# A DeltaNet / RWKV-7 / PEER decoder step: RWKV matrices directly behind the z tiles, gate tiles redistributed, inversion units by chunk

## Time and profile before

| | |
|---|---|
| runs shown | 1148.66 (median), 1147.56, 1153.62 us |
| the profiled execution's own time | 1150.32 us |
| its span | 1148.6 us |
| PE busy | 982.6 us (86%) |
| DVE busy | 706.5 us (62%) |
| POOL busy | 521.4 us (45%) |
| ACT busy | 264.1 us (23%) |
| mean granted TensorE clock | 0.978 of full |

### The profile page before, as it was taken

How to read it: one execution, slowest core, us unless ns; L and a number is a source line. 1 busy time by engine, 2 the same in 40 slices (tenths; PEclk the granted TensorE clock), 3 DMA queues, 4 the chain that set the end, 5 groups by cost and what they waited for, 6 DMA issues and landing times.

```text
span 1148.6 us, 11115 instructions
## 1 busy us (share of the span) xinstructions
PE 982.6 (86%) x3667; PEld 549.7 (48%) x3667; DVE 706.5 (62%) x1870; ACT 264.1 (23%) x635; POOL 521.4 (45%) x583
## 2 busy tenths in 40 slices
PE   6999998999999998988987777777777777777787
PEld 5886676889987447654442222222222222222221
DVE  2025862983466338883775775776686676677543
ACT  2147544023251012220131111111122111111111
POOL 2000100000000016577577677777767777777763
PEclk9998989998999998998999999999999999999999
DMA  9342022463165319999999999999999999999996
GB/s 288 110 153 74 1 76 50 135 171 82 40 208 208 110 46 405 407 371 353 409 406 403 409 409 409 406 408 408 408 388 410 409 409 410 405 409 404 395 371 263
DMA packets 121862, 334.24 MB, mean 291 GB/s; under 512 B 19119, under 2 KB 36370, under 8 KB 121542
## 3 DMA queue, kind: packets, MB, share of 16 engines
q0 software_dynamic: 76032, 276.86, 61.2%
q1 hardware_dynamic: 45642, 56.64, 15.2%
q10 hardware_dynamic: 132, 0.04, 0.0%
HBM read 326.99 MB, written 5.74 MB: 290 GB/s over the span
## 4 chain that ended last, share of the span: by engine, by line
PE 31%; DMA 28%; DVE 23%; POOL 9%; issue 5%; ACT 3%; ACTq 0%; DVEq 0%; POOLq 0%
PE bank L1428 29%; DMA sb_all<-in_peer_u,idx 22%; POOL sb_all L591 9%; DMA sb_all<-in_peer_v,idx 6%; DVE sb_all L1148 6%; ACT sb_all L1846 2%; DVE sb_all L1126 1%; DVE sb_all L1124 1%; DVE sb_all L1128 1%; DVE sb_all L2337 1%; DVE sb_all L2334 1%; DVE key_i L1096 1%; DVE sb_all L1089 1%; ACT L1846 1%; DVE key_i L1090 1%
## 5 line engine op out<-in xcount | busy, mean ns | idle before, releaser
L1428 PE MATMUL bank<-sb_all 128*128 128x512 f32 (+19 forms) x3390 | 952.3, 433 | 145.8 <-DMA sb_all<-in_peer_v,idx 135.6
L1428 PEld LDWEIGHTS bank<-sb_all 128*128 128x128 f32 (+8 forms) x3390 | 522.9, 182 | 569.7 <-DMA sb_all<-in_peer_v,idx 320.4
L1148 DVE CUSTOM_DVE_ANT_0 sb_all<-sb_all,bank 128x1024 f32<-128x1024 f32 x264 | 314.8, 1220 | 186.5 <-DMA sb_all<-in_peer_u,idx 186.0
L591 POOL DMA_INDIRECT sb_all<-in_peer_u,idx x264 | 252.6, 957 | 212.4 <-issue 161.1
L591 POOL DMA_INDIRECT sb_all<-in_peer_v,idx x264 | 254.6, 965 | 88.8 <-issue 63.8
L1846 ACT ACTIVATE sb_all<-sb_all 128x128 f32<-128x128 f32 (+9 forms) x367 | 145.1, 421 | 561.7 <-PE bank L1428 368.6
L1846 ACT ACTIVATE sb_all<-bank 128x264 f32<-128x264 f32 (+18 forms) x175 | 76.7, 455 | 305.2 <-PE bank L1428 272.0
L627 POOL MEMSET sb_all<- 128x512 f32 x1 | 0.5, 524 | 140.9 <-PE bank L1428 140.9
L1418 POOL MEMSET sb_all<- 128x3456 f32 x1 | 3.0, 2984 | 129.1 <-DVE sb_all L2248 129.1
L2129 DVE SCALAR_TENSOR_TENSOR sb_all<-sb_all 128x288 f32<-128x288 f32 x14 | 6.1, 514 | 61.2 <-ACT sb_all L1846 61.2
L1846 ACT ACT_TABLE_LOAD x22 | 28.2, 1283 | 7.5 <-DVE sb_all L2269 3.9
(11 more groups left out here) (237 smaller groups left out, 403.5 us busy)
## 6 DMA issues: line engine op xcount, KB each, us to landing
sb_all<-in_w_in SPq DMA_DIRECT2D x8, 2048.0 KB, 8.1
sb_all<-in_peer_wq SPq DMA_DIRECT2D x4, 2048.0 KB, 17.3
sb_all<-in_w_in SPq DMA_DIRECT2D x6, 1024.0 KB, 4.9
sb_all<-in_peer_u,idx POOLq DMA_INDIRECT x264, 10.8
sb_all<-in_peer_v,idx POOLq DMA_INDIRECT x264, 11.0
out<-sb_all SPq DMA_DIRECT2D x8, 512.0 KB, 3.9
sb_all<-in_w_out SPq DMA_DIRECT2D x2, 2048.0 KB, 8.6
sb_all<-in_x_prompt SPq DMA_DIRECT2D x4, 512.0 KB, 4.4
```

The lines of the kernel that those rows point to most:

```text
L591: pool.indirect_dma_start(ring[at % 8], None, table[0], bass.IndirectOffsetOnAxis(ap=idx[:, c:c + 1], axis=0)).then_inc(landed[at % 8], 16)
L1148: v.tensor_tensor_reduce(uring[i % 8], uring[i % 8], x, 1.0, 0.0, ALU.mult, ALU.add, hdot[:, u % 2, j:j + 1]).then_inc(u_free, 1)
L1428: return nc.tensor.matmul(out, lhsT, rhs, start=start, stop=stop, **kw)
```

## The change

- **z tiles.** z tile 1 is split: two of its products behind each group of decay products, the last two behind the second of the four key products. Sample rows are turned between the key/query matrices. z tile 2 follows the sample rows, then the token rows go through banks 0 to 5 (those of the key/query matrices), then z tile 3.
- **RWKV matrices** begin directly behind z tile 3. The RWKV rows are turned one set at a time in front of matrices 7 to 12. The first six products with bb follow, then the key sum, half a gate tile, the last six products, and the rest of the gate tiles.
- **Gate tiles.** 12 tiles (g0, g1, g2) are under the substitution; the four of g3 come behind it: tile 0 behind the first right side, tile 1 behind DeltaNet's first u, tiles 2 and 3 where they were. g3 is loaded in one transfer once g2 is used up. Tile 0's sigmoid moves to `act_rest`.
- **Inversion.** Units go by chunk (all three g of chunk 0 first), and the last `inv_twice` stands behind the first g3 tile. The first right side needs only unit 6's result.
- **DVE.** The copy of chunk 0's v into `r_buf` goes; PE reads v directly. The copy of the key sum moves behind all masks.

```diff
-        UNITS_INV = [(g, q) for g in range(3) for q in range(3)]
+        UNITS_INV = [(g, q) for q in range(3) for g in range(3)]
...
-        IN_PARTS = {"g1": (256,), "g2": (256,), "g3": (128, 128)}
+        IN_PARTS = {"g1": (256,), "g2": (256,)}
...
+        svt_t, prw_t = series(sem("rows_t"), 6, 6)
...
+            step(fn(gates(12), gates(12), ACT.Sigmoid))
...
-        FILL = [(name, f) for name in ("g0", "g1", "g2") for f in range(4)] + [("g3", 0), ("g3", 1)]
+        FILL = [(name, f) for name in ("g0", "g1", "g2") for f in range(4)]
...
+            def z_tile(f, b, first, last):
+
+                slot = wait_w(pe, "z")
+                for k in range(first, last):
+                    ins = mm(psv(b, 128, NX), wslot[slot][:, k, f * 128:(f + 1) * 128], xnT[:, k, T0:NC],
+                             start=k == 0, stop=k == KT - 1)
+                if last == KT:
+                    ins.then_inc(proj_ready, 1)
+                    tile[0] += 1
+
+            def key_back(f):
+
+                pe.wait_ge(qk_mul.sem, qk_mul.at(f + 1))
+                mm(psv(f, 128, NC), to_rows[0:8, 4 + f, :], qk_norm[0:8, :]).then_inc(k_back.sem, 1)
...
             pe.wait_ge(gb_in, 2)
+            pe.wait_ge(proj_used, 27)
             for c in range(NCH):
                 for h in range(DH):
                     ins = mm(psv((4, 5, 7)[c], 128, TC, at=TC * h), gbc[0:TC, 4 * c + h, :], incl[0:TC, :])
                 ins.then_inc(gb_ready.sem, 1)
-            for f in range(4):
-                pe.wait_ge(qk_mul.sem, qk_mul.at(f + 1))
-                mm(psv(f, 128, NC), to_rows[0:8, 4 + f, :], qk_norm[0:8, :]).then_inc(k_back.sem, 1)
+                z_tile(1, 6, 2 * c, 2 * c + 2)
+            key_back(0)
+            key_back(1)
+            z_tile(1, 6, 6, KT)
+            key_back(2)
+            key_back(3)
+
...
+                if x >= 2:
...
-            project("z", T0, banks=4, part=(1, 2))
-
...
                     h = 2 * hp + s
                     ins = mm(psv(n, TC, 2, TC, at=2 * TC * s), qkv[:, 4 + h, ccols(c)], qkv[:, h:h + 5:4, ccols(c)])
                 ins.then_inc(kq_ready.sem, 1)
...
+                if n == 1:
+                    pe.wait_ge(proj_used, 28)
+                    pe.wait_ge(rw_vec_ready, 1)
+                    pe.wait_ge(exp2_ready.sem, exp2_ready.at(2))
+                if n >= 1:
+                    sample_rows(n - 1)
+            sample_rows(5)
+
+            pe.wait_ge(svt_ready.sem, svt_ready.at(5))
+            z_tile(2, 6, 0, KT)
             for n in range(6):
-                if n < 2:
-                    pe.wait_ge(svt_ready.sem, svt_ready.at(5 + n))
-                else:
-                    pe.wait_ge(tok_ready.sem, tok_ready.at(n - 1))
+                pe.wait_ge(kq_used, n + 1)
                 c, kv = n // 2, n % 2
                 for f in range(4):
-                    ins = nc.tensor.transpose(psv(6 + kv, TC, 128, at=128 * f), qkv[:, 4 + 4 * kv + f, ccols(c)], ident)
+                    ins = nc.tensor.transpose(psv(n, TC, 128, at=128 * f), qkv[:, 4 + 4 * kv + f, ccols(c)], ident)
                 ins.then_inc(tok_t.sem, 1)
...
-            pe.wait_ge(rw_vec_ready, 1)
-            for n in range(6):
-                if n >= 2:
+            pe.wait_ge(svt_ready.sem, svt_ready.at(6))
+            z_tile(3, 7, 0, KT)
+
...
+            def rw_rows(n):
+
...
+                if n < 2:
+                    pe.wait_ge(proj_used, 29 + n)
+                else:
                     pe.wait_ge(prw_ready.sem, prw_ready.at(n - 1))
                 c, src = n // 2, (bb, kb)[n % 2]
                 for f in range(4):
                     ins = nc.tensor.transpose(psv(6 + n % 2, TC, 128, at=128 * f), src[:, f, ccols(c)], ident)
                 ins.then_inc(prw_t.sem, 1)
 
-            pe.wait_ge(kq_used, 6)
-            project("z", T0, banks=4, part=(3, 4))
-
...
-            pe.wait_ge(proj_used, 30)
             for n in range(12):
-                if n >= 6:
+                if n < 6:
+                    pe.wait_ge(tok_ready.sem, tok_ready.at(n + 1))
+                else:
+                    rw_rows(n - 6)
                     pe.wait_ge(rwm_used, n - 5)
                 rw_matrix(n % 6, kb, n // 6, n % 6 // 2, n % 2).then_inc(rwm_ready.sem, 1)
...
+            for n in range(6):
+                pe.wait_ge(rwm_used, n + 7)
+                rw_matrix(n, bb, 0, n // 2, n % 2).then_inc(rwb_ready, 1)
             pe.wait_ge(prw_ready.sem, prw_ready.at(6))
-            fill_tile(0, KT // 2)
-            pe.wait_ge(rwm_used, 12)
             pe.wait_ge(kqp_ready, 1)
             mm(psv(7, 128, 32), ones, sdv[:, 2, :]).then_inc(kq_sum.sem, 1)
-            for g in (1, 2):
-                for n in range(6):
-                    if g == 1:
-                        pe.wait_ge(rwm_used, 12)
-                    else:
-                        pe.wait_ge(rwb_used, n + 1)
-                    rw_matrix(n, bb, g - 1, n // 2, n % 2).then_inc(rwb_ready, 1)
+            fill_tile(0, KT // 2)
+            for n in range(6):
+                pe.wait_ge(rwb_used, n + 1)
+                rw_matrix(n, bb, 1, n // 2, n % 2).then_inc(rwb_ready, 1)
             fill_tile(KT // 2, KT)
...
-                    pe.wait_ge(proj_used, 43)
+                    pe.wait_ge(proj_used, 42)
...
-            for u in range(NU + 3):
-                if u < NU:
-                    inv_turn(u)
-                if 1 <= u < NU + 1:
-                    inv_left(u - 1)
-                if 2 <= u < NU + 2:
-                    inv_once(u - 2)
-                if u >= 3:
-                    inv_twice(u - 3)
-
-            pe.wait_ge(proj_used, 43)
...
-            pe.wait_ge(inv_z_used, NU)
+            for u in range(NU + 2):
+                if u < NU:
+                    inv_turn(u)
+                if 1 <= u < NU + 1:
+                    inv_left(u - 1)
+                if u >= 2:
+                    inv_once(u - 2)
+                if u >= 3:
+                    inv_twice(u - 3)
+            pe.wait_ge(inv_z_used, 7)
+            right_side(0).then_inc(rw_r, 1)
+            pe.wait_ge(inv_x_used, NU)
+            gate_tile(0, 0)
+            inv_twice(NU - 1)
             for c in range(NCH):
-                if c == 0:
-                    right_side(0).then_inc(rw_r, 1)
-                else:
+                if c > 0:
+                    if c == 1:
+                        pe.wait_ge(proj_used, 43)
                     pe.wait_ge(dn_s_done, c)
                     for h in range(DH):
...
-                pe.wait_ge(dn_r_done, c + 1)
+                if c > 0:
+                    pe.wait_ge(dn_r_done, c)
                 for h in range(DH):
-                    ins = mm(psv(1, TC, 128, at=128 * h), xTm(4 * c + h), r_buf[0:TC, 128 * h:128 * h + 128])
+                    r_h = r_buf[0:TC, 128 * h:128 * h + 128] if c > 0 else v_dn[0:TC, 0, 128 * h:128 * h + 128]
+                    ins = mm(psv(1, TC, 128, at=128 * h), xTm(4 * c + h), r_h)
                 ins.then_inc(dn_u, 1)
+                if c == 0:
+                    gate_tile(1, 3)
                 pe.wait_ge(rw_r_done, c + 1)
-                pe.wait_ge(proj_used, (44, 45, 46)[c])
+                pe.wait_ge(inv_z_used, NU)
+                pe.wait_ge(proj_used, (42, 45, 46)[c])
                 for h in range(RH):
...
+                if c == 0:
+                    pe.wait_ge(proj_used, 44)
...
-            evacuate(zs[1:2], ACT.Silu, NX, banks=4)
+
+            def z_out(f, b):
+
+                act.wait_ge(proj_ready, 27 + f)
+                fn(zs[f], psv(b, 128, NX), ACT.Silu).then_inc(proj_used, 1)
+                tile[0] += 1
+
+            z_out(1, 6)
...
-                act.wait_ge(svt_t, x + 1)
...
+            z_out(2, 6)
...
+                        ins = fn(k_dn[0:TC, c, 128 * h:128 * h + 128], psv(n, TC, 128, at=128 * h),
...
+                    ins = fn(v_dn[0:TC, c, :], psv(n, TC, 512))
...
-            evacuate(zs[2:3], ACT.Silu, NX, banks=4)
+            z_out(3, 7)
...
-            evacuate(zs[3:4], ACT.Silu, NX, banks=4)
-            for n in range(len(FILL) - 1):
+            for n in range(len(FILL)):
...
-            act.wait_ge(inv_sum.sem, inv_sum.at(NU))
             act.wait_ge(inv_c, NU)
...
-            act.wait_ge(yv_ready, 1)
-            act.wait_ge(strw_sent, 32)
-            gate_out(1, 7)
             for c in range(NCH):
                 act.wait_ge(rw_r, c + 1)
                 fn(r_bufw[0:TC], psv(4, TC, 512)).then_inc(rw_r_done, 1)
+                if c == 0:
+                    gate_out(0, 0)
+                    act.wait_ge(inv_sum.sem, inv_sum.at(NU))
+                    gate_out(1, 3)
+                    act.wait_ge(yv_ready, 1)
+                    act.wait_ge(strw_sent, 32)
...
-            dve.wait_ge(kq_sum.sem, kq_sum.at(1))
-            v.tensor_copy(sdv[:, 2, :], psv(7, 128, 32)).then_inc(kq_copied, 1)
...
+            dve.wait_ge(kq_sum.sem, kq_sum.at(1))
```

(40 more changed lines are left out.)

18 lines of the change are left out of this document (removed).

## The result

**1168.63 us** against 1148.11 us, medians of four runs each; ratio 1.0158, 95% interval 1.0125 to 1.0192: slower by 18 us. The forecast was 1162.3 with a range up to 1169, so the time lies 6.3 us above the one and 0.4 us inside the other. The mechanism is the one forecast: the inversion ran at half clock. The profiled execution took 1168.72 us (span 1166.8 us; before 1150.32 and 1148.6), 18.4 more.

The account below looks back on a forecast made before the run. No engine bounds the whole kernel; the touched stretch is a serial DVE and PE chain. -3.0 us at full clock plus 14.2, 1.1 and 1.3 at half clock gave +13.6: 1163.9 profiled, 1162.3 us median, range 1146 to 1169.

Parts of the forecast that it names:

- The gap and the clock: Between gate tiles and inversion: PE idle from 241.8 to about 249, short turns until 250.8, so the clock drops.
- A wait that was put at nothing: Key-sum copy on DVE moved behind the masks: claimed to cost nothing.
- The price of the inversion: Inversion's small products at half clock: 18.0 us stretched by factor 1.79, costing 14.2 us.
- Right side and gate tile: Behind the inversion at low clock: 1.1 us for the right side, 1.3 for the gate tile's first part.
- At full clock the change would gain: Up to the o product, if the clock held: 282.8 against 285.75, -3.0 us.
- The sum: Whole change: -3.0 at full clock plus 14.2, 1.1 and 1.3 for the low clock, +13.6 us.
- the forecast's own case: Clock low through the inversion until the gate tile behind it: +13.6 us, bounds 1157.6 to 1166.1; chance 60%.
- rival 3: Front: z tile fails to hold the clock among thin products, first matrix about 4 us later; +17.6, 1166.3 us; 12%.
- the upper price: Upper bound for the inversion at half clock: all its products double, 18.0 us instead of 14.2.
- Rival 1: Inversion: clock comes back early, costing 2.0 us, units of 2.0 us by the third; -1.0, 1147.7 us; 20%.
- Mis-sized on the front: RWKV matrices: 0.65 us each on PE, 1.13 per pair of rows and matrix; last mask done at 204.0.
- Queues: DMA queues: state transfers land at 200.5, hidden under masks ending 204.0; g1 wanted at 213, just in time.

Follow-up runs that it names:

- front_half: Changed kernel's front alone, with the back half of the kernel before (fourteen gate tiles under the substitution): 1147.53 us, ratio 0.9979 to before.
- drain: Changed kernel with fourteen gate tiles under the substitution, the fifteenth behind the first right side, the sixteenth at chunk 1's end: 1140.81 us, ratio 0.9914 to before.
- warm: Changed kernel plus twelve unused 128-row products on PE before its wait for the inverse blocks: 1148.12 us, ratio 0.9978 to before.
- warm_thin: Changed kernel plus eleven unused 8-row products on PE before its wait for the inverse blocks: 1167.46 us, ratio 1.0159 to before.
- late_tiles: Changed kernel, last two gate tiles under the substitution held until its last rows are sent: median 1167.40 us, one of four runs 1144.09.
- back_half: Front of the kernel before with the changed kernel's back half alone (twelve gate tiles under the substitution): 1167.45 us, ratio 1.0140 to before.
- thirteen: Changed kernel with thirteen gate tiles under the substitution instead of twelve, no added products: 1160.44 us, ratio 1.0099 to before.
- revive: Changed kernel plus twelve unused 128-row products inside the inversion, ahead of the fifth unit's turn: 1158.32 us, ratio 1.0069 to before.

## Why the prediction was right

- **The gap and the clock.** Forecast: PE without work from 241.8 to about 249 and on to 250.8. Measured, less the 2.2 us of the late start: 243.9 to 248.4, on to 250.7. The waits were 4.55 and 0.77 us, not 7.2 and then two short turns, because the last tile ended 2.1 us later than forecast and the blocks came 0.6 sooner; they were enough.
- **A wait that was put at nothing.** The key-sum copy behind the masks was to cost nothing. But the second gate tile waits for it (`kq_copied`): the copy is done at 206.24, the tile starts at 206.34, and PE has stood 1.53 us. That is most of the 2.1; eleven tiles in 39.75 us for 39.2 are the rest. All ten kernels with the new front show this wait (1.52 or 1.53 us). In the changed kernel it hides in the gap and makes it smaller. In front_half and drain the tiles set the inversion's start, so it may cost there; no run moves the copy back.
- **The price of the inversion.** Forecast 14.2 (factor 1.79 on 18.0 us); measured 33.2 against 18.5, that is 14.7, factor 1.80. The row of sixteen 64-column products was the right one to take. The 18.0 ends at PE's last product, the 18.5 at the eighth add. The step from add to add is 3.88 us at half and 2.16 at full clock; the forecast had 3.6 and 2.0, as it divided 18.0 by nine and so spread the shorter last steps over all.
- **Right side and gate tile.** Forecast 1.1 and 1.3. In the changed kernel they take 288.92 - 286.11 = 2.81 and 293.76 - 288.92 = 4.84 us, in warm 1.56 and 3.56: 1.25 and 1.28.
- **At full clock the change would gain.** Forecast -3.0. warm is the changed kernel with its clock held: from the copy of z tile 0 to the first o copy it takes 130.30 us (152.37 to 282.67), before 133.94 (151.81 to 285.75), so 3.6 less. The ratio, 0.9978 [0.9956, 0.9999], says 2.5 us with 0.1 to 5 possible.
- **The sum.** Forecast +13.6. By ACT's copy behind the first o product it is 17.0 (302.79 and 285.75), of which 2.2 existed before the change: 14.8. So the terms up to there came out 1.2 short, 1.0 of it in the inversion, which took 33.2 where 18.0 + 14.2 were forecast. At 341.16 it is still 17.0 (324.12 before). The rest, to 18.4 between the profiled executions, comes right behind, above all in the sample state's products: 9.8 us at 343.94, of which the first 5.4 at half clock, against 8.71 before and 7.2 in warm. Why the clock fell there in this run and not in warm wasn't tested.
- **What was luck.** The 1168.63 lies above the bounds of the forecast's own case (1157.6 to 1166.1) and inside the range only because the range reached up to 1169. By the forecast's numbers the end named for it, rival 3 with the upper price, is 1166.3 + 3.8 = 1170.1. The 6.3 us between 1162.3 and the measured median are, but for rounding, these 1.2, the 2.2 of a late start ahead of anything that the change touches, 1.4 behind 341 us, and 1.6 by which the forecast was lowered from profiled execution to median, while here the two agree.
- **Rival 1, the clock back early in the inversion,** is refuted: up to 37 us of small products at 0.50 (warm_thin, late_tiles). The Trainium skill (TensorE: Matmul & The Clock Gate, Part 1), which the prediction cited, has sustained matmul activity bring full clock back after a few us and asks for no shape. This trace disagrees: PE was busy for all of 33.2 us and the clock stayed at 0.50. The measurement decides.
- **Rival 3, the z tile doesn't hold the clock,** came in part. The clock was 1.00 from 155 to 165, as forecast, but fell right behind and stayed low among the key/query matrices and sample rows. The first mask came at 186.79, or 184.6 less the late start, where 181.5 was forecast. Of the ten profiled kernels with the new front, the stretch took some 3.4 us in seven and 6.8 in three, this one among them; the old front has 10.2 (before, back_half). The longer stretch is worth 1.4 of the 3.1 us: the first mask comes 31.3 to 31.6 us behind the copy of z tile 0 in the seven, 32.8 to 32.9 in the three, and 29.7 was forecast.
- **Mis-sized on the front.** Six bb matrices in a row pass PE faster than the 0.65 us each that I took (DVE masks them 0.53 us apart, from 197.06 on, and never waits), and a pair of turned row set and matrix takes 1.39 us (195.02 less 193.63 in the timeline below), not 1.13. These and the later first mask cancel: the last mask is done at 206.06, less 2.2, 203.9, for a forecast of 204.0. That this number came out is luck.

```profile
193.63 0.64 PE L1637 MATMUL bank<-sb_all 128*96 128x128 f32 x4
...
195.02 0.64 PE L1637 MATMUL bank<-sb_all 128*96 128x128 f32 x4
```

- **Queues.** The last state transfer went out at 197.98 + 1.18 and took 6.1 us to land: 205.3, just ahead of the last mask at 205.80, where 3.5 us were forecast to be spare. g1 was in time for its tiles.

## What to carry to other kernels

When PE runs a chain of small products, look at what stands directly ahead of it. Work that fills PE up to the last wait isn't only cover for that wait; it carries the clock into the chain, and moving it away can cost far more than its own length. Price such a move by the granted clock of the windows on both sides, not by PE's busy share. Where nothing useful can fill a gap of a few us, wide products with an unused result are cheap insurance, if they reach up to the end of the wait: twelve did here, six didn't. Where a chain is already slow, wide products placed inside it help too. When a copy moves behind other work, look for everyone who waits for it. And run a kernel whose gap is on the edge several times, since it can fall on either side.

## What the runs showed of the hardware

- The inversion's small products neither lowered the clock nor raised it: the same 96, 64 and 32-column products ran 18.5 us at 1.00 when wide products led up to them (warm, drain), and 33 us at 0.50 when a gap did. Whether their rows or their columns matter wasn't tested.
- Waits of 1.41 and 0.62 us (thirteen) lost the clock for over 34 us; 0.34 to 0.38 us (drain, warm) didn't, nor did the 1.03 us of the kernel before. These kernels differ in more than the wait, so the figures give no limit.
- Products of 8 rows didn't hold it: 1.00 fell to 0.50 at 244.0 in warm_thin with PE busy 8.6 us of 8.6.
- Wide products brought it back 3.4 us after it fell in late_tiles. In revive the clock was 1.00 at 263.80; the added products stand behind 24 small ones that began at 257.69 and take 3.3 us, so they had run for about 2.8 us.
